# Expert gate and up projections turned over: weight blocks stationary, routed tokens streamed, in the mixture-of-experts stage of a two-layer decoder

## Chip, cores and metric

The kernel runs on one core of one Trainium2 chip. The metric is the device time of one execution in microseconds (us); lower is better. Before the change the median of three runs is 1061.97 us (1061.96 to 1063.9).

## What is computed

256 tokens of width 1024 pass through two layers, all in float32. Each layer has a token mixer (three attention branches and an output projection) and a feed-forward part. In layer 0 that is a dense SwiGLU of width 2816, in layer 1 a choice of two out of eight SwiGLU experts of width 1408. Only the expert stage is touched by the change:

```python
h = rms_norm(x, norm2_g[1])
logits = h @ w_router                       # 256 x 8
top_v, top_i = lax.top_k(logits, 2)
top_p = softmax(top_v)
combine = sum(one_hot(top_i, 8) * top_p[..., None], axis=1)
for e in range(8):
    out += combine[:, e:e+1] * ((silu(h @ w_gate[e]) * (h @ w_up[e])) @ w_down[e])
```

`w_gate` and `w_up` are 1024 x 1408 for each expert, `w_down` is 1408 x 1024. The eight experts hold 138.4 MB of weights.

## The kernel before

The mixer and the dense stage split each operand into a high and a low part of type float32r (three products instead of one) and take two thirds of the time. They are not changed. Then the router's logits are computed (two products per 128-row block, the token block stationary and 8 columns streamed), DVE turns them into slot numbers, and the expert stage begins.

**Passes.** The expert stage does two experts at a time, a heavy one with up to `HEAVY` = 96 token slots and a light one with up to `LIGHT` = 64. A loop with a count computed on the chip takes further passes if an expert has more tokens than slots; the kernel runs `STATIC` = 2 passes unrolled, then a loop, then the last pass written out by itself. With these inputs there are four passes.

**Gather.** `gather` (PE, line 1958) multiplies the 0/1 matrix `sel` (token to slot) with the token rows, kept as float32r high and low parts: 32 matmuls, each with a 128x128 block of the rows stationary and 160 slots streamed. ACT (`gathered`, line 918) copies the result to `xe`, feature-major, with the norm's gain.

**Gate and up.** `hidden(half, q, i)` (PE, line 1989) runs over two halves of the expert width (704 columns) and four pairs of 128-row blocks of the model width. The tokens are stationary and the weights are streamed. `quads` (line 1983) gives each of four 32-column strips of the array a group of 32 slots, so that four matmuls run side by side, each streaming 352 weight columns:

```python
for g in range(4):
    ins = plain(ps[g * OV:(g + 1) * OV, bank, 0:w], lhsT[:, g * OV:(g + 1) * OV], rhs[g // 2], first, last)
```

That covers 128 of the 160 slots. The last 32 slots of the heavy expert (the overflow) are four more strips, over 384 and 320 weight columns. ACT applies the SiLU with the norm factor of each slot as its scale (`gated`), DVE multiplies with the up product and again the factor. The products lie slot-major in `ehid` and `ehid2`.

**Turns.** The down projection needs them feature-major. `turn0` (line 2030) does 12 transposes on PE (8 of products, 4 of `sel`), `turn1` (line 2049) nine more; DVE copies them to `ehT`, `ehT2`, `selT`.

**Down and scatter.** `down` (line 2087) has 32 slots stationary and 512 weight columns streamed, again as quads. The result is scaled by the combine weight, split in high and low, and `scatter` (line 1972) adds it to the tokens by matmuls with `selT`; it runs in the first steps of the next pass (in pass 0 it runs on zeros). In the last pass all of the left output half (`h` = 0) is computed ahead of most of the right half, so that its scaling and scatter lie beside matmuls.

**Weights.** SP issues every weight load into one ring, `e_ring`, of three chunks (half a pass). A load waits for `e_used`, which PE raises after each step of `hidden` and `down`. A gate or up unit is 704 KB, a down unit 512 KB. The first 24 units are loaded during the mixer.

A matmul on plain float32 appears in the trace as two records, each with its own weight load (LDWEIGHTS, "PEld") and matmul; one on float32r appears as one.

Of the kernel before, what the change touches and what calls it, by code (L numbers as in the profile page):

```python
# [27 lines left out]
P = 128  # L28
# [173 lines left out]
HEAVY, LIGHT = 96, 64  # L202
OV = HEAVY - LIGHT
SLOTS = HEAVY + LIGHT
LISTED = 8
POSITIONS = NE + LISTED
WANT = (0, 5, 1, 4, 2, 3)
HALF_E = FE // 2
SLAB = HALF_E // 2
OV_SLAB = 384  # L210
OV_CUTS = (((0, 384, 0), (384, 320, 0)), ((0, 320, 64), (320, 384, 0)))
TURNED = 5
# [11 lines left out]
CHUNK = 8 * 2 * HALF_E  # L224
# [4 lines left out]
def e_place(u):  # L229

    turn, at = (0, u) if u < 24 else (1, u - 24)
    if turn == 0 or at < 8:
        chunk, j, size = at // 8, at % 8, 2 * HALF_E
    else:
        chunk, j, size = 1 + (at - 8) // FET, (at - 8) % FET, D
    if chunk == 2:
        return CHUNK_AT[2] + CHUNK - size * (j + 1), size
    return CHUNK_AT[chunk] + size * j, size


def e_before(u):

    a, n = e_place(u)
    here = [v for v in range(len(E_UNITS)) if (v < 24) != (u < 24) and e_place(v)[0] < a + n and a < sum(e_place(v))]
    return max(here)


E_FREE_LATER = (((0, 1, 2, 3, 4, 5, 16, 17), "v"), ((6, 7, 8, 9, 10, 11, 12, 13, 14, 15), "y"), ((18, 19), "wo"),
                ((20, 21), "router"), ((22, 23), "counts"))


E_GROUP = [u // 4 for u in range(len(E_UNITS))]
# [45 lines left out]
def build(nc, t):  # L298
    with ExitStack() as ctx:
# [28 lines left out]
        def expert_buffers():  # L328
# [5 lines left out]
                "ehid": sb("ehid", [FE]), "ehid2": sb("ehid2", [OV_SLAB]),  # L334
                "ehT": sb("ehT", [FET, P]), "ehT2": sb("ehT2", [FET, OV]),
                "y_hi": sb("y_hi", [D], F32R), "y_lo": sb("y_lo", [D], F32R),
                "y2": sb("y2", [2, HALF], F32R),
                "sg": sb("sg_e", [2, SLAB]), "sg2": sb("sg2_e", [OV_SLAB]),
# [21 lines left out]
        pslots, pscale = sb("pslots", [TT, POSITIONS + 2]), sb("pscale", [TT, POSITIONS + 2, 4], F32R)  # L360
# [63 lines left out]
        ehid, ehid2, ehT, ehT2 = eb["ehid"], eb["ehid2"], eb["ehT"], eb["ehT2"]  # L424
        y_hi, y_lo, y2 = eb["y_hi"], eb["y_lo"], eb["y2"]
        sg_e, sg2_e = eb["sg"], eb["sg2"]
# [3 lines left out]
        spare_sg = sg_e[:, :, :].rearrange("p a b -> p (a b)")  # L430
# [26 lines left out]
        loaded_e = [sem(f"loaded_e{i}") for i in range(len(E_UNITS) // 2)]  # L457
# [22 lines left out]
        turn0_filled, turn0_read = sem("turn0_filled"), sem("turn0_read")  # L480
        turn1_filled, turn1_read = sem("turn1_filled"), sem("turn1_read")
# [19 lines left out]
        def e_unit(u):  # L501

            _, _, _, k, _, c = E_UNITS[u]
            at, size = e_place(u)
            return e_ring[:, at:at + size].rearrange("p (k c) -> p k c", k=k)

# [50 lines left out]
        def _(sp):  # L557
# [10 lines left out]
            def expert_load(u, experts):  # L568
                which, e, k0, k, c0, c = E_UNITS[u]
                src = block_of(t["experts"][experts[e]], expert_at[which, k0, k, c0, c], k, c)  # L570
                sp.dma_start(e_unit(u), src).then_inc(loaded_e[u // 2], 16)
# [3 lines left out]
            for n, (src, k, w) in enumerate(static_units):  # L575
                if n == early_at:
                    sp.wait_ge(aux_done, FIRST[1, ("V3", 0)][2] + 2)
                if early_at <= n < early_at + len(free_later["v"]):
                    expert_load(free_later["v"][n - early_at], (0, 1))
# [25 lines left out]
            for u in range(24, len(E_UNITS)):  # L605
                sp.wait_ge(e_used, E_GROUP[e_before(u)] + 1)
                expert_load(u, (0, 1))
            sp.wait_ge(route_ready, 1)
            iters = sp.value_load(ids[0:1, POSITIONS:POSITIONS + 1], min_val=NE // 2, max_val=POSITIONS // 2)
            with sp.Fori(1, iters) as i:  # L610
                experts = [sp.value_load(ids[0:1, bass.ds(i * 2 + e, 1)], min_val=0, max_val=NE - 1) for e in range(2)]
                for u in range(len(E_UNITS)):
                    at = E_GROUP[e_before(u)] + 1 - (E_GROUPS if u < 24 else 0)
# [10 lines left out]
        def _(pool):  # L624
# [54 lines left out]
            pool.wait_ge(w_used, UNITS0)  # L679
            pool.memset(one[:, :, :], 0.0)  # L680
            for at, r in enumerate(WANT):
                pool.memset(want[:, at:at + 1], float(r))
            pool.memset(selT[:, :, :].bitcast(F32), 0.0)
            pool.memset(y_hi[:, :].bitcast(F32), 0.0)
            pool.memset(y_lo[:, :].bitcast(F32), 0.0)
            pool.memset(y2[:, :, :].bitcast(F32), 0.0).then_inc(moe_zero, 1)
# [9 lines left out]
        def _(act):  # L696
# [221 lines left out]
            def gathered(i):  # L918

                for g in range(3):  # L920
                    act.wait_ge(xe_filled, i * 3 + g + 1)
                    for k in range(3 * g, min(3 * g + 3, KD)):
                        at = (k - 3 * g) * SLOTS
                        ins = act.activation(xe[:, k, :], ps[:, 2 + g, at:at + SLOTS], ACT.Copy,
                                             scale=gain[:, 3 * KD + k:3 * KD + k + 1])
                    ins.then_inc(xe_ready, 1)

            gathered(0)
            act.wait_ge(diff_ready, 1)
            act.activation(ti[:, 5, :], ti[:, 4, :], ACT.Exp).then_inc(e_ready, 1)  # L930
            act.wait_ge(iters_ready, 1)
            last = act.value_load(ids[0:1, POSITIONS + 1:POSITIONS + 2], min_val=NE // 2 - 1, max_val=POSITIONS // 2 - 1)

            def gated(i):

                act.wait_ge(scale_ready, i + 1)
                for half in range(2):
                    for s in range(2):
                        act.wait_ge(hid_filled, i * 4 + 2 * half + s + 1)
                        act.activation(sg_e[:, s, :], ps[:, 2 * s, 0:SLAB], ACT.Silu, scale=slot_scale[:, 1:2]).then_inc(sg_ready, 1)  # L940
                    act.wait_ge(e_used, i * E_GROUPS + KQ * (half + 1))
                    act.activation(sg2_e[2 * OV:4 * OV, :], ps[0:2 * OV, 4, 0:OV_SLAB], ACT.Silu,
                                   scale=slot_scale[0:2 * OV, 3:4]).then_inc(sg_ready, 1)

# [11 lines left out]
            def full_pass(i):  # L956

                gated(i)
                gathered(i + 1)
# [6 lines left out]
            for i in range(STATIC):  # L966
                full_pass(i)
            with act.Fori(STATIC, last) as i:
# [3 lines left out]
            sqrt_table()  # L972
            act.wait_ge(y_filled, last * 2 + 1)
# [7 lines left out]
            act.activation(ehid[:, 0:HALF], ps[:, 6, :], ACT.Copy, scale=slot_scale[:, 0:1]).then_inc(y_hi_ready, 1)  # L981
# [14 lines left out]
        def _(dve):  # L996
# [328 lines left out]
            for n in range(3):  # L1325
                dve.memset(spare[:, n:n + 1], 0.0).then_inc(y_split, 1)
            for n in range(2):
                dve.memset(spare[:, 3 + n:4 + n], 0.0).then_inc(turn1_read, 1)
# [15 lines left out]

            def select(slot):

                dve.tensor_tensor(sel[:, :, 0:P].rearrange("p t (e c) -> p t e c", e=2),
                                  iota[:, 1:LIGHT + 1].unsqueeze(1).unsqueeze(1).broadcast_to([P, TT, 2, LIGHT]),
                                  slot(0, 2).unsqueeze(3).broadcast_to([P, TT, 2, LIGHT]), ALU.is_equal)
                dve.tensor_tensor(sel[:, :, P:2 * P].rearrange("p t (g c) -> p t g c", g=4),  # L1350
                                  iota[:, LIGHT + 1:HEAVY + 1].unsqueeze(1).unsqueeze(1).broadcast_to([P, TT, 4, OV]),
                                  slot(0, 1).unsqueeze(3).broadcast_to([P, TT, 4, OV]), ALU.is_equal).then_inc(sel_ready, 1)

# [4 lines left out]
            select(lambda n, w: eslot[:, :, n:n + w])  # L1358
# [4 lines left out]
            mean_square(3)  # L1363

# [10 lines left out]
            link(dve.tensor_scalar(heavy, rank, 2.5, float(OV), ALU.is_lt, ALU.mult))  # L1375
# [34 lines left out]


            dve.wait_ge(mean_sq, 4)
            rsqrt(nrm[:, 4, :], nrm[:, 3, :], nrm[:, 5, :], root, 4)
            scale18 = nrm[:, 4, :].unsqueeze(2).broadcast_to([P, TT, POSITIONS + 2])
            link(dve.tensor_copy(pscale[:, :, :, 2], scale18))
            link(dve.tensor_tensor(pscale[:, :, :, 3], scale18, pscale[:, :, :, 2].bitcast(F32), ALU.subtract))
# [42 lines left out]
            dve.wait_ge(iters_ready, 1)  # L1459
            last = dve.value_load(ids[0:1, POSITIONS + 1:POSITIONS + 2], min_val=NE // 2 - 1, max_val=POSITIONS // 2 - 1)  # L1460

# [9 lines left out]
            def scales(i):  # L1471

                dve.wait_ge(scale_filled, i + 1)
                for rows, dst, at in ((slice(0, LIGHT), 0, 0), (slice(LIGHT, P), 0, 4), (slice(0, P), 2, 8)):
                    ins = dve.tensor_reduce(slot_scale[rows, dst:dst + 2].unsqueeze(2),
                                            ps[rows, 6, at:at + 4].rearrange("p (v s) -> p v s", s=2), AX.X, ALU.add)
# [3 lines left out]
            def hidden(i, half):  # L1480

                c0 = half * HALF_E
                for s in range(2):
                    dve.wait_ge(sg_ready, i * 6 + 3 * half + s + 1)
                    dve.scalar_tensor_tensor(out=ehid[:, c0 + s * SLAB:c0 + (s + 1) * SLAB], in0=ps[:, 2 * s + 1, 0:SLAB],
                                             scalar=slot_scale[:, 1:2], in1=sg_e[:, s, :],
# [714 lines left out]
```

## Time and profile before

| | before |
|---|---|
| median of 3 runs | 1061.97 us |
| the profiled execution, its own time | 1068.14 us |
| its span | 1066.4 us |
| PE busy / PE weight loads busy | 1050.6 us (99%) / 867.3 us (81%) |
| DVE busy / ACT busy | 518.9 us (49%) / 402.5 us (38%) |
| mean granted TensorE clock | 0.983 of full |
| read from memory | 252.93 MB |

The span runs from the first to the last instruction. PE's busy time is a union of overlapping matmuls whose ends are modelled, so 99% says that PE always had something in flight, not that it ran at its peak. The weight loads are listed as an engine of their own since they overlap the matmuls. A granted clock of 1.00 is 2.4 GHz, one of 0.50 is 1.2 GHz.

### The profile page before, as it was taken

The page shows a single profiled execution, that of the slowest core. Times are in us where ns is not written, and L with a number is a line of the kernel's source. Part 1 is how long each engine was busy: PE and PEld are TensorE (multiplying, and loading weights), DVE is VectorE, ACT ScalarE, POOL GpSimd, SP SyncE. Part 2 cuts the span into 40 slices and gives each one's busy share as a digit, 9 for nine tenths or more (in the row PEclk, how much of TensorE's full clock was granted, in tenths as well). Part 3 has the DMA queues.
Part 4 walks back from the last instruction along what each step waited for, and adds up shares of the span by engine and source line. Part 5 has one row for each costly group of instructions (what it writes and reads, how often), then busy time and mean ns, then how long its engine had stood idle before and what let it go on. Part 6 is the DMA issues. An engine that isn't in the chain of part 4 may idle for free.

```text
span 1066.4 us, 21967 instructions
## 1 busy us (share of the span) xinstructions
PE 1050.6 (99%) x9653; PEld 867.3 (81%) x9653; DVE 518.9 (49%) x751; ACT 402.5 (38%) x619; POOL 16.2 (2%) x61
## 2 busy tenths in 40 slices
PE   7999999999999999999999999999999999999996
PEld 7998999999999999999899999995654554563552
DVE  4566676577467565465577755954112111111112
ACT  5553655636354353447356564431111011011012
POOL 3000000000000000000000000010000000000000
PEclk8999999999999999999999999988999999999998
DMA  6543543556455465454435348895999999999961
GB/s 213 173 154 93 177 157 137 171 188 204 152 179 184 153 221 189 167 172 155 138 106 191 131 130 308 311 386 212 406 414 414 409 413 414 411 411 415 411 271 40
DMA packets 56910, 255.38 MB, mean 239 GB/s; under 512 B 7505, under 2 KB 7537, under 8 KB 56818
## 3 DMA queue, kind: packets, MB, share of 16 engines
q1 hardware_dynamic: 55954, 252.41, 64.5%
q8 instruction: 76, 1.25, 0.5%
q10 hardware_dynamic: 864, 1.59, 0.4%
q14 instruction: 16, 0.13, 0.0%
HBM read 252.93 MB, written 1.05 MB: 238 GB/s over the span
## 4 chain that ended last, share of the span: by engine, by line
PE 95%; DMA 2%; DVE 1%; ACT 1%; issue 0%; ACTq 0%; DVEq 0%
PE ps L1603 37%; PE ps L1598 16%; PE ps L1600 16%; PE ps L1599 16%; PE ps L1592 3%; PE ps L1594 3%; PE ps L1593 3%; DMA raw<-in_dense 1%; PE ps L1811 1%; DMA x<-in_x 1%; ACT w_hi L708 0%; DVE w_lo L1008 0%; PE ps L2036 0%; PE ps L2045 0%; PE ps L2053 0%
## 5 line engine op out<-in xcount | busy, mean ns | idle before, releaser
L1008 DVE TENSOR_TENSOR w_lo<-raw,w_hi 128x1536 fp32r<-128x1536 f32 (+2 forms) x157 | 248.1, 1604 | 128.6 <-ACT w_hi L708 128.4
L708 ACT ACTIVATE w_hi<-raw 128x1536 fp32r<-128x1536 f32 (+2 forms) x157 | 210.4, 1361 | 155.4 <-DMA raw<-in_dense 153.5
L1598 PE MATMUL ps<-hT_hi,w_hi 128*128 128x256 f32 (+1 forms) x752 | 216.3, 288 | 4.2 <-DVE hT_lo L1057 4.2
L1600 PE MATMUL ps<-hT_hi,w_lo 128*128 128x256 f32 (+1 forms) x752 | 213.0, 283 | 0.0
L1599 PE MATMUL ps<-hT_lo,w_hi 128*128 128x256 f32 (+1 forms) x752 | 212.9, 283 | 0.0
L1603 PE MATMUL ps<-e_ring,xe 128*32 128x352 f32 (+2 forms) x2560 | 199.9, 463 | 0.0
L1603 PEld LDWEIGHTS ps<-e_ring,xe 128*32 128x32 f32 x2560 | 106.1, 110 | 83.5 <-issue 56.2
L1598 PEld LDWEIGHTS ps<-hT_hi,w_hi 128*128 128x128 f32 (+1 forms) x752 | 142.4, 189 | 8.5 <-issue 7.6
L1600 PEld LDWEIGHTS ps<-hT_hi,w_lo 128*128 128x128 f32 (+1 forms) x752 | 142.4, 189 | 0.4
L1599 PEld LDWEIGHTS ps<-hT_lo,w_hi 128*128 128x128 f32 (+1 forms) x752 | 142.2, 189 | 0.4
L1603 PE MATMUL ps<-e_ring,ehT 128*32 128x512 f32 x880 | 101.1, 593 | 0.0
L1598 PE MATMUL ps<-h_hi,w_hi 128*128 128x256 f32 x352 | 100.1, 284 | 0.6 <-DVE w_lo L1008 0.6
L1600 PE MATMUL ps<-h_hi,w_lo 128*128 128x256 f32 x352 | 99.1, 282 | 0.0
L1599 PE MATMUL ps<-h_lo,w_hi 128*128 128x256 f32 x352 | 99.0, 281 | 0.0
L1603 PEld LDWEIGHTS ps<-e_ring,ehT 128*32 128x32 f32 x880 | 32.8, 110 | 59.3 <-issue 53.8
L940 ACT ACTIVATE sg_e<-ps,slot_scale 128x352 f32<-128x352 f32 x16 | 8.9, 553 | 168.5 <-PE ps L1603 168.5
L1598 PEld LDWEIGHTS ps<-h_hi,w_hi 128*128 128x128 f32 x352 | 67.0, 190 | 0.8 <-DVE w_lo L1008 0.8
L1599 PEld LDWEIGHTS ps<-h_lo,w_hi 128*128 128x128 f32 x352 | 66.9, 190 | 0.0
L1600 PEld LDWEIGHTS ps<-h_hi,w_lo 128*128 128x128 f32 x352 | 66.9, 190 | 0.0
L1592 PE MATMUL ps<-w_hi,hT_hi 128*128 128x256 f32 (+1 forms) x208 | 64.6, 311 | 0.1
L1594 PE MATMUL ps<-w_hi,hT_lo 128*128 128x256 f32 (+1 forms) x208 | 63.9, 307 | 0.0
L1593 PE MATMUL ps<-w_lo,hT_hi 128*128 128x256 f32 (+1 forms) x208 | 63.7, 306 | 0.0
(330 smaller groups left out, 1419.4 us busy)
## 6 DMA issues: line engine op xcount, KB each, us to landing
e_ring<-in_experts SPq DMA_DIRECT2D x128, 704.0 KB, 11.5
raw<-in_dense SPq DMA_DIRECT2D x112, 768.0 KB, 4.3
e_ring<-in_experts SPq DMA_DIRECT2D x88, 512.0 KB, 10.3
raw<-in_dense SPq DMA_DIRECT2D x42, 512.0 KB, 3.6
raw<-in_dense SPq DMA_DIRECT2D x3, 544.0 KB, 3.9
raw<-in_dense SPq DMA_DIRECT2D x2, 272.0 KB, 3.6
x<-in_x ACTq DMA_DIRECT2D x2, 256.0 KB, 6.6
x<-in_x SPq DMA_DIRECT2D x1, 512.0 KB, 8.6
```

The source lines that it names most:

```text
L708: act.activation(slot(n, "hi", k), slot(n, "raw", k), ACT.Copy).then_inc(hi_done, 1)
L940: act.activation(sg_e[:, s, :], ps[:, 2 * s, 0:SLAB], ACT.Silu, scale=slot_scale[:, 1:2]).then_inc(sg_ready, 1)
L1008: dve.tensor_tensor(slot(n, "lo", k), slot(n, "raw", k), slot(n, "hi", k).bitcast(F32), ALU.subtract).then_inc(lo_done, 1)
L1592: pe.matmul(out, hi, wh, start=first, stop=False, skip_group_check=True)
L1593: pe.matmul(out, hi, wl, start=False, stop=False, skip_group_check=True)
L1594: return pe.matmul(out, lo, wh, start=False, stop=last, skip_group_check=True)
L1598: pe.matmul(out, wh, hi, start=first, stop=False, skip_group_check=True)
L1599: pe.matmul(out, wh, lo, start=False, stop=False, skip_group_check=True)
L1600: return pe.matmul(out, wl, hi, start=False, stop=last, skip_group_check=True)
L1603: return pe.matmul(out, lhsT, rhs, start=start, stop=stop, skip_group_check=True)
L1811: ins = pe.transpose(aux_bank(a + hh)[:, blk * P:(blk + 1) * P], sm[:, at:at + P], ident[:, :])
```

## The change

Gate and up are turned over. A unit of weights now holds, for one expert and one half, 2 row blocks of 11 column blocks of 128: five gate blocks, five up blocks, and one block that is half gate and half up (64 columns each). Each block is the stationary operand, and the slots of that expert are streamed: 84 for the heavy one, 64 for the light one. The products come out feature-major, so they need no turn. `HEAVY` falls from 96 to 84 and the slots from 160 to 148.

```diff
-HEAVY, LIGHT = 96, 64
-OV = HEAVY - LIGHT
+HEAVY, LIGHT = 84, 64
+OV = 32
+GATED = FE // P // 2
+GU = (2 * GATED + 1) * P
...
-        E_UNITS += [(which, e, 2 * _q, 2, HALF_E * _h, HALF_E) for which in ("gate", "up") for e in range(2)]
+        E_UNITS += [("hidden", e, 2 * _q, 2, _h, GU) for e in range(2)]
...
             def hidden(half, q, i):
-                for s in range(2):
...
-                        for kk, k in enumerate(ks):
-                            ins = quads(2 * s + kind, SLAB, xe[:, k, 0:P], [units[2 * kind + e][:, kk, cols] for e in range(2)],
-                                        k == 0, k == KD - 1)
...
+                for e in range(2):
+                    n, at = WIDTH[e], AT[e]
+                    u = (half * KQ + q) * 2 + e
+                    weights = e_unit(u)
+                    if half == 1 and q == 0:
+                        pe.wait_ge(hid_ready, i * 4 + e + 1)
+                    expert_ready(u, i)
+                    for kk in range(2):
...
+                        for b in range(2 * GATED + 1):
+                            bank, j = (2 * e + 1, b - GATED) if GATED <= b < 2 * GATED else (2 * e, min(b, GATED))
+                            ins = plain(ps[:, bank, j * n:(j + 1) * n], weights[:, kk, b * P:(b + 1) * P], xe[:, k, at:at + n],
+                                        k == 0 and j == 0, k == KD - 1)
```

The norm factor of a token no longer enters at the SiLU. After the first of its three groups, `gather` does two more float32 matmuls that put the factor of each slot on all partitions (`r_rows` times `sel`), and the copy to `xe`, now on DVE, multiplies by it:

```diff
+                    if g == 0:
+                        if first:
+                            pe.wait_ge(r_ready, 1)
+                        for tt in range(TT):
+                            ins = plain(ps[:, 1, 0:SLOTS], r_rows[:, tt, :], sel[:, tt, 0:SLOTS].bitcast(F32), start=tt == 0, stop=tt == TT - 1)
+                        ins.then_inc(r_filled, 1)
```

Of the turns only the four transposes of `sel` stay (`turn`, before step (1, 1)); `turn0` and `turn1` go. ACT applies the SiLU to five blocks at once and to the half block, DVE multiplies straight into `ehT`:

```diff
-                ins.then_inc(turn1_filled, 1)
...
+            def turn(i, first):
+
+                if not first:
+                    pe.wait_ge(added, i * 4 + 4)
+                pe.wait_ge(sel_all, i + 1)
+                for part in range(2):
+                    for tt in range(TT):
+                        ins = pe.transpose(ps[:, 7, (2 * part + tt) * P:(2 * part + tt + 1) * P],
+                                           sel[:, tt, part * P:(part + 1) * P].bitcast(F32), ident[:, :])
+                ins.then_inc(turn_filled, 1)
```

Three smaller edits go with it. Pass 0 has no scatter and no add of rows any more. In the last pass the two output halves are computed side by side, and the last block decides both:

```diff
-            for k in range(4):
+            for k in range(FET):
                 down_ready(k, last)
                 down_main(k, 0)
-            turn1(last)
-            for k in range(4):
+                if k == FET - 1:
+                    down_over((k,)).then_inc(y_filled, 1)
                 down_main(k, 1)
...
+                if k < FET - 1:
+                    down_over((k,))
+            pe.wait_ge(y_split, last * 3 + 2)
```

And SP issues a pass's gate and up weights as 16 loads of 1408 KB instead of 32 of 704 KB; the bytes are the same. In the mixer these early loads stand at every second dense load.

## Rows read from the trace of the kernel before

**Rows 1.** The page: span, busy time by engine, GB/s in 40 slices.

```profile
span 1066.4 us, 21967 instructions
...
PE 1050.6 (99%) x9653; PEld 867.3 (81%) x9653; DVE 518.9 (49%) x751; ACT 402.5 (38%) x619; POOL 16.2 (2%) x61
...
GB/s 213 173 154 93 177 157 137 171 188 204 152 179 184 153 221 189 167 172 155 138 106 191 131 130 308 311 386 212 406 414 414 409 413 414 411 411 415 411 271 40
```

**Rows 2.** The page's DMA issues: count, KB each, us to landing.

```profile
e_ring<-in_experts SPq DMA_DIRECT2D x128, 704.0 KB, 11.5
...
e_ring<-in_experts SPq DMA_DIRECT2D x88, 512.0 KB, 10.3
```

**Rows 3.** Chain that ended last, in order: start us, us, engine, line.

```profile
867.17 57.77 PE ps L1603 x614
...
950.19 57.77 PE ps L1603 x614
```

**Rows 4.** Timeline of PE in pass 0: start us, us, line, operands, records.

```profile
723.03 7.85 PE L1603 MATMUL ps<-e_ring,xe 128*32 128x352 f32 x80
...
730.81 0.51 PE L1603 MATMUL ps<-y_hi,selT 128*128 128x512 f32 x1
...
733.11 6.22 PE L1603 MATMUL ps<-e_ring,xe 128*32 128x352 f32 x80
```

**Rows 5.** The same view, later in pass 0.

```profile
739.26 0.50 PE L1603 MATMUL ps<-y_hi,selT 128*128 128x512 f32 x1
...
740.16 6.22 PE L1603 MATMUL ps<-e_ring,xe 128*32 128x352 f32 x80
746.31 0.61 PE L1603 MATMUL ps<-pscale,sel 128*128 128x8 f32 x4
746.85 12.04 PE L1603 MATMUL ps<-e_ring,xe 128*32 128x352 f32 x160
758.82 0.66 PE L2036 MATMUL ps<-ident,ehid 128*128 128x128 f32 x4
...
760.43 17.63 PE L1603 MATMUL ps<-e_ring,xe 128*32 128x352 f32 x236
...
782.93 0.66 PE L2053 MATMUL ps<-ident,ehid 128*128 128x128 f32 x4
...
784.07 4.50 PE L1603 MATMUL ps<-e_ring,ehT 128*32 128x512 f32 x40
788.50 3.80 PE L1603 MATMUL ps<-sel,rows 128*128 128x160 f32 x32
792.23 15.21 PE L1603 MATMUL ps<-e_ring,ehT 128*32 128x512 f32 x137
```

**Rows 6.** Timeline: runs of matmuls with 128 stationary columns.

```profile
709.36 2.31 PEld L1603 LDWEIGHTS ps<-r_gain,xhat 128*128 128x128 f32 x20
709.46 2.30 PE L1603 MATMUL ps<-r_gain,xhat 128*128 128x8 f32 x20
...
716.01 7.09 PE L1603 MATMUL ps<-sel,rows 128*128 128x160 f32 x32
```

**Rows 7.** Sums by stretch; PEclk is the first number after the engines.

```profile
700.00:712.00 12.00, 12.00 (x102) 12.00 (x102) 4.29 (x15) 5.01 (x15) 3.48 (x11) 1.00 0.98 381
712.80:722.80 10.00, 10.00 (x49) 10.00 (x48) 8.14 (x47) 2.13 (x7) 0.00 (x0) 0.50 0.91 347
722.80:726.40 3.60, 3.60 (x26) 1.28 (x29) 1.96 (x13) 2.16 (x4) 0.00 (x0) 0.51 0.03 13
726.40:740.00 13.60, 13.60 (x152) 6.44 (x144) 5.63 (x20) 0.00 (x0) 0.00 (x0) 1.00 0.55 214
...
790.00:792.00 2.00, 2.00 (x20) 2.00 (x20) 0.00 (x0) 1.52 (x5) 0.00 (x0) 1.00 1.02 417
```

**Rows 8.** Timeline of ACT in the tail of the last pass.

```profile
1054.88 0.69 ACT L981 ACTIVATE ehid<-ps,slot_scale 128x512 f32<-128x512 f32 x1 [1.30 <-PE ps L1603]
```

More of the change, by code:

```diff
@@ L199 @@
 BANKS = 4
-HEAVY, LIGHT = 96, 64
-OV = HEAVY - LIGHT
+HEAVY, LIGHT = 84, 64
+OV = 32
 SLOTS = HEAVY + LIGHT
+WIDTH = (HEAVY, LIGHT)
+AT = (LIGHT, 0)
 LISTED = 8
@@ L243, in e_before @@
     a, n = e_place(u)
-    here = [v for v in range(len(E_UNITS)) if (v < 24) != (u < 24) and e_place(v)[0] < a + n and a < sum(e_place(v))]
+    here = [v for v in range(len(E_UNITS)) if (v < TURN) != (u < TURN) and e_place(v)[0] < a + n and a < sum(e_place(v))]
     return max(here)
-E_FREE_LATER = (((0, 1, 2, 3, 4, 5, 16, 17), "v"), ((6, 7, 8, 9, 10, 11, 12, 13, 14, 15), "y"), ((18, 19), "wo"),
-                ((20, 21), "router"), ((22, 23), "counts"))
-E_GROUP = [u // 4 for u in range(len(E_UNITS))]
+E_FREE_LATER = (((0, 1, 2, 8), "v"), ((3, 4, 5, 6, 7), "y"), ((9,), "wo"), ((10,), "router"), ((11,), "counts"))
+E_GROUP = [u // 2 if u < DOWN_AT else (u - DOWN_AT) // 4 + DOWN_AT // 2 for u in range(len(E_UNITS))]
 E_GROUPS = E_GROUP[-1] + 1
@@ L456, in build @@
         loaded = [sem(f"loaded{i}") for i in range(RING)]
-        loaded_e = [sem(f"loaded_e{i}") for i in range(len(E_UNITS) // 2)]
+        loaded_e = [sem(f"loaded_e{i}") for i in range(DOWN_AT + FET)]
         hi_done, lo_done, w_used = sem("hi_done"), sem("lo_done"), sem("w_used")
@@ L604, in _ @@
                 expert_load(u, (0, 1))
-            for u in range(24, len(E_UNITS)):
+            for u in range(TURN, len(E_UNITS)):
                 sp.wait_ge(e_used, E_GROUP[e_before(u)] + 1)
@@ L972, in _ @@
             sqrt_table()
+            act.wait_ge(scale_ready, last + 1)
             act.wait_ge(y_filled, last * 2 + 1)
@@ L1322, in _ @@
                         split_lo(u)
[L1325 to L1328, printed above, removed]
+            for n in range(4):
+                dve.memset(spare[:, n:n + 1], 0.0).then_inc(added_filled, 1)
+                dve.memset(spare[:, n + 4:n + 5], 0.0).then_inc(added, 1)
             a = ROUTER_AUX
@@ L1342, in _, with matches @@
             rows_lo(2)
-            def select(slot):
[L1347 to L1352, printed above, removed]
+            def matches(first, n, out, slots):
+                shape = list(out.shape)
+                numbers = iota[:, first:first + n].unsqueeze(1)
+                if len(shape) == 4:
+                    numbers, slots = numbers.unsqueeze(1), slots.unsqueeze(3)
+                return dve.tensor_tensor(out, numbers.broadcast_to(shape), slots.broadcast_to(shape), ALU.is_equal)
+            def select(slot):
+                matches(1, HEAVY, sel[:, :, LIGHT:SLOTS], slot(0))
+                matches(1, LIGHT, sel[:, :, 0:LIGHT], slot(1)).then_inc(sel_ready, 1)
+                matches(LIGHT + 1, HEAVY - LIGHT, sel[:, :, P + OV:2 * P].rearrange("p t (g c) -> p t g c", g=3)[:, :, :, 0:HEAVY - LIGHT],
+                        slot(0)).then_inc(sel_all, 1)
             a += 1
@@ L1480, in hidden @@
             def hidden(i, half):
[L1482 to L1486, printed above, removed]
-                                             op0=ALU.mult, op1=ALU.mult).then_inc(hid_ready, 1)
-                dve.wait_ge(sg_ready, i * 6 + 3 * half + 3)
@@ L1549, in _ @@
             add_rows(last)
+            hidden(last, 0)
+            turned(last)
             scales(last)
-            hidden(last, 0)
-            turned0(last)
             hidden(last, 1)
-            turned1(last)
             dve.wait_ge(y_hi_ready, last * 4 + 1)
@@ L1980, in expert_ready @@
             def expert_ready(u, i):
-                pe.wait_ge(loaded_e[u // 2], i * 32 + 32)
+                per_pass = 16 if u < DOWN_AT else 32
+                pe.wait_ge(e_loaded(u), i * per_pass + per_pass)
             def quads(bank, w, lhsT, rhs, first, last):
                 for g in range(4):
-                    ins = plain(ps[g * OV:(g + 1) * OV, bank, 0:w], lhsT[:, g * OV:(g + 1) * OV], rhs[g // 2], first, last)
+                    ins = plain(ps[g * OV:(g + 1) * OV, bank, 0:w], lhsT[:, g * OV:(g + 1) * OV], rhs[1 - g // 2], first, last)
@@ L2093, in down, with first_half, second_half @@
                 down_over(k_pair(q)).then_inc(e_used, 1)
-            def first_half(i):
-                pe.wait_ge(turn1_read, i * 2 + 2)
+            def first_half(i, first=False):
                 hidden(0, 0, i)
-                pe.wait_ge(y_split, i * 3 + 3)
-                for g in range(3):
-                    scatter(g)
+                if not first:
+                    pe.wait_ge(y_split, i * 3)
+                    for g in range(3):
+                        scatter(g)
                 hidden(0, 1, i)
-                pe.wait_ge(added, i * 4 + 1)
-                scatter(3)
+                if not first:
+                    pe.wait_ge(added, i * 4 + 1)
+                    scatter(3)
                 hidden(0, 2, i)
+                hidden(0, 3, i)
+            def second_half(i, first=False):
+                hidden(1, 0, i)
+                turn(i, first)
                 pe.wait_ge(scale_known, 1)
                 slot_scales(i)
-                hidden(0, 3, i)
-            def second_half(i):
-                hidden(1, 0, i)
-                turn0(i)
                 hidden(1, 1, i)
@@ L2166, in _ @@
                 out, tokens = ps[:, LAST_BANKS[1][tt], :], slice(tt * P, (tt + 1) * P)
-                plain(out, selT[:, 0, tokens].bitcast(F32), ehid[:, 0:HALF], stop=False)
+                plain(out, selT[:, 0, tokens].bitcast(F32), y_last[:, :], stop=False)
                 plain(out, selT[:, 1, tokens], y2[:, 1, :], start=False).then_inc(added_filled, 1)
@@ L2188, with gate_up @@
     laid["dense"] = np.concatenate([cut(given[w][l], *block) for w, l, *block in dense_blocks()])
-    laid["experts"] = np.stack([np.concatenate([cut(given["moe_w_" + w][0, e], *block) for w, *block in expert_blocks()]) for e in range(NE)])
+    def gate_up(e, h):
+        gate, up = given["moe_w_gate"][0, e], given["moe_w_up"][0, e]
+        wide, narrow = slice(GATED * P * h, GATED * P * (h + 1)), slice(2 * GATED * P + 64 * h, 2 * GATED * P + 64 * (h + 1))
+        return np.concatenate([gate[:, wide], up[:, wide], gate[:, narrow], up[:, narrow]], axis=1)
+    laid["experts"] = np.stack([np.concatenate([cut(gate_up(e, h), k0, k, 0, c) if w == "hidden" else cut(given["moe_w_down"][0, e], k0, k, h, c)
+                                                for w, k0, k, h, c in expert_blocks()]) for e in range(NE)])
     laid["x"] = np.asarray(inputs["x"])[0].T.reshape(KD, P, T).transpose(1, 0, 2)
```

266 lines of the change are left out of this document (105 added, 161 removed).

## The prediction

> **What bounds the kernel now.** I read the page first. PE has work in flight for 1050.6 of 1066.4 us, DVE and ACT for half or less [rows 1]; so only PE's own time counts, unless memory does. In the last third of the span the memory moves 406 to 415 GB/s without a dip [rows 1], which asks whether the expert stage is bound by its loads. The chain that ended last answers: one down stage begins at 867.17 and the next at 950.19, so a pass takes 83.0 us, and the chain runs through PE alone [rows 3]. The loads of a pass are 32 of 704 KB and 22 of 512 KB [rows 2], 34.6 MB, and 34.6 MB in 83.0 us are 417 GB/s. PE and memory are in balance: a faster PE would soon run into its loads, a slower one just stretches the pass.
>
> I then add up PE's pass from the timeline, to see that no wait hides in it. A step of `hidden` (80 records) takes 6.15 us, from 733.11 to 739.26 [rows 4, 5] and again from 740.16 to 746.31; two take 11.97 us, three 17.46 us (760.43 to about 777.9) [rows 5]. Three single steps, the two and the three make 8 steps and 47.9 us. The turns take 1.61 us (758.82 to 760.43) and 1.14 us (782.93 to 784.07), the slot scales 0.54 us, the gather 3.73 us (788.50 to 792.23) [rows 5]. The scatters take 2.30 us (730.81 to 733.11) and 0.90 us (739.26 to 740.16) [rows 4, 5]. The down projection has 220 records, 40 of them take 4.43 us (784.07 to 788.50) [rows 5], so 24.4 us. The sum is 82.5 us of 83.0: PE waits for nothing.
>
> **The step that decides: what one record of the new gate and up costs.** The new `hidden` has per pass 2 halves x 8 row blocks x 11 column blocks x 2 experts = 352 matmuls in float32, which are 704 records, each with a load of 128 stationary columns of its own. The old one has 640 records with 32 stationary columns, four side by side. So I look for runs of records with 128 stationary columns at full clock. With 8 columns streamed, 20 records start over 2.30 less one record's length of about 0.25 us: 19 steps, 0.108 us each, at a clock of 1.00 [rows 6, 7]. With 160 streamed, 32 records take 3.73 us, 0.117 us each to the next instruction or 0.113 us between their own starts (3.80 less about 0.3, over 31) [rows 5], also at 1.00 [rows 7]. Twenty times as many streamed columns cost 5 to 9 ns: the load of 128 stationary columns sets the pace, not the stream. The new records stream 84 or 64 float32 columns. An old step has 20 groups of four records, with 7168 columns one behind the other (16 x 352 and 4 x 384) in 6.15 us, so at most 0.86 ns a column; 84 columns are then 0.072 us and 64 are 0.055 us, both below 0.108. So a new record takes between 0.108 us (8 columns) and 0.117 us (160 columns); I take 0.111. A pass has 704 x 0.111 = 78.1 us in place of 47.9.
>
> The Trainium skill (TensorE: Matmul & The Clock Gate, section Back-to-back issue gap) gives about 81 ns per matmul for a sustained stream of load and matmul pairs with 128 streamed columns. By that a pass would have 704 x 0.081 = 57.0 us and the change would cost far less. The rows disagree, 0.108 us even with 8 columns, and the same page (section Weight-path perf modes) says that the fast weight load is not used for FP32. It stands below as a rival.
>
> **The clock.** At half clock the same load takes twice as long: the first gather's 32 records take 7.09 us, 0.215 us from start to start (7.09 less about 0.43, over 31) [rows 6], at 0.50 [rows 7]. It fell at 712.8, behind the logits with their 8 columns and the short waits around them [rows 6, 7]. From there the gather runs without a break to 722.8 and the clock stays at 0.50; with 3.6 us of quads it is back at 1.00 [rows 7]. The new `hidden` starts right behind this gather, and its records are of the gather's kind: a load of 128 columns each, and a stream that is shorter than the load. So I take it that in pass 0 it stays at half clock to its end, and that the down quads bring the clock back. In pass 0's second gather the same kind of records ran for 3.7 us from full clock, and it stayed at 1.00 [rows 5, 7]. So I take the later passes at full clock, with less certainty: their `hidden` lasts 78 us, not 3.7.
>
> **The sum.** Against the profiled span of 1066.4 us (own time 1068.14), which the median of the runs shown, 1061.97, undercuts by 6.2 us; I add the difference to the median.
>
> Pass 0. Removed: `hidden`, whose first step took 7.78 us (723.03 to 730.81) since part of it ran at half clock [rows 4], so 49.5; the scatters on zeros, 3.2; of the turns 8 of 12 transposes and all of the second, 1.07 + 1.14 = 2.2. Together 54.9. Added: 704 x 0.215 = 151.4; the factor's 4 records, 1.0 at half clock; the four transposes and slot scales at half clock, 1.1 more; the first part of the down projection at half clock, 2.5 (bounds 1.7 to 3.6, from the 3.6 us that quads needed [rows 7]). Net +101.1. Before it, the factor's records stand in the gather: +1.1; the copies to `xe` are now DVE's, about 0.3 us each behind the last group, and only the first group is waited for at once.
> Passes 1 and 2, each: 78.1 + 0.5 (factor) - 47.9 - 2.2 = +28.5, together +57.0.
> Last pass: 78.1 - 47.9 - 2.2 = +28.0.
> Tail. Before, scaling, split and scatter of the left half lay beside the right half's matmuls; the last scaling on ACT (0.69 us) began at 1054.88 and 11.5 us led from it to the end [rows 8]. Now some seven such operations stand between the last down block and that point, with 1 us of matmuls left beside them: +4 (2 to 6).
> Sum: 101.1 + 1.1 + 57.0 + 28.0 + 4.0 = +191 us, so 1253 us.
>
> At no cost: SiLU and products, since each of them has the other expert's records of a step (44 x 0.111 = 4.9 us) beside it before PE needs the bank or `ehT`; without that cover about 1.5 us for each of four per pass. The next pass's `select` and the copies to `xe` lie beside the down projection, with some 15 us to spare. The loads: 34.6 MB in 111 us are 312 GB/s, so PE no longer meets them; loads twice as large in the mixer could hold a dense load up once or twice (0 to 2 us). More passes would come if an expert had more tokens than slots, but the reference's router gives 71, 53, 72, 58, 59, 66, 59 and 74 tokens, with 84 slots for each of four and 64 for the others: four passes as before.
>
> **Rivals.**
> (a) The clock returns soon in pass 0. For it: PE has no pause in `hidden`. Against: nor has the gather. Pass 0 then has 78.1 + 0.5 + 3.5 (its first 7 us at half clock) - 54.9 = +27.2; total 27.2 + 1.1 + 57.0 + 28.0 + 4.0 = +117, 1179 us. Chance 0.14.
> (b) The clock falls in passes 1 to 3 too, where 64 columns are streamed, and stays down to the end of `hidden`. For it: the fall at 712.8 followed records with few columns. Against: the warm gather. Each of three passes has 73.3 + about 6 (scatters, turn, first quads) more than above: +429, 1491 us. Chance 0.10; a fall in some passes only, 1290 to 1450, another 0.05.
> (c) The loads hide behind the stream, and a record takes its stream: 352 x 0.072 + 352 x 0.055 = 44.7 us a pass, -4.9 us with the turns and the factor. This ends on the other side. The place is every `hidden` step, and it decides below (47.9 + 2.2 - 0.5) / 704 = 0.070 us a record. PE alone would give about 1042 us (-9.7 + 1.1 - 2 x 4.9 - 5.4 + 4.0); as memory already moves what 83 us need, more likely 1050 to 1062. Against: the rows with 128 stationary columns are all at 0.108 us or more. Chance 0.02.
> (d) A record takes 0.081 us, by the page named above: 57.0 + 0.5 - 50.1 = +7.4 a pass. With pass 0 at twice that (0.162) the total is about +91, 1153 us; all at full clock, about 1095. Chance 0.02.
> The forecast has 0.67, its own range 1235 to 1275: +-5 ns on the 2112 records at full clock is 10 us, the rest waits and tail.
>
> **How the numbers follow.** The likeliest case gives 1253. To hold the time 8 times in 10 the range takes in (a): low 1170, high 1285. That leaves out (b), (c) and (d) and the partial falls, 0.19. This measurement can tell about 0.2%, 2 us. Only (c) is near or under the old time: faster 0.01, same 0.01, slower 0.98.
>
> **What the profile of the changed kernel would show.** The record spacing: groups of 44 records of `ps<-xe,e_ring` with 128 stationary columns, 4.9 us each, PE's weight loads busy throughout. The clock: 0.50 from about 713 to 876, then 1.00; a pass distance of about 111 us; memory near 312 GB/s in passes 1 to 3. Wrong would be a spacing under 0.105, a clock of 1.00 within pass 0's `hidden`, or 0.50 in later ones.

## The result, and the profile after

The changed kernel is slower: 1174.06 us in the median of five runs against 1062.46 us, a ratio of 1.103 with a 95% interval of 1.100 to 1.106. The forecast was 1253 us with a range of 1170 to 1285. Its runs lie on two levels: two of the five took 1251.34 and 1253.14 us, three took 1173.15 to 1174.06, and the ratio is made from the latter. The profiled execution is one of the former, 1253.14 us with a span of 1251.4. What separates the levels is the subject of most of the experiments.

The page of the changed kernel: span, busy time, the granted clock in tenths and the memory rate in 40 slices.

```profile
span 1251.4 us, 22172 instructions
...
PE 1232.5 (98%) x9845; PEld 1139.5 (91%) x9845; DVE 514.2 (41%) x765; ACT 389.9 (31%) x595; POOL 13.3 (1%) x59
...
PEclk8999999999999999999999855555999999999998
...
GB/s 207 177 119 160 147 133 180 177 198 178 178 152 219 178 165 165 144 133 144 146 220 319 370 125 102 177 137 140 331 317 270 345 356 257 296 344 345 277 102 34
```

Against [rows 1], the weight loads on PE rise from 867 to 1140 us, and memory no longer stands at 406 to 415 GB/s in the expert stage: it moves 102 to 177 GB/s in pass 0 and swings between 257 and 356 in the passes behind it. Five slices at half clock, which the kernel before did not have, follow the router.

The timeline of PE in the changed kernel (start us, us, line, operands, records), pass by pass:

```profile
723.56 94.06 PE L1594 MATMUL ps<-xe,e_ring 128*128 128x84 f32 x440
817.41 1.06 PE L2026 MATMUL ps<-ident,sel 128*128 128x128 f32 x4
...
818.98 56.56 PE L1594 MATMUL ps<-xe,e_ring 128*128 128x84 f32 x264
875.47 10.59 PE L1594 MATMUL ps<-e_ring,ehT 128*32 128x512 f32 x80
...
905.79 10.04 PE L1594 MATMUL ps<-xe,e_ring 128*128 128x84 f32 x88
...
928.33 29.59 PE L1594 MATMUL ps<-xe,e_ring 128*128 128x84 f32 x264
957.76 0.60 PE L2026 MATMUL ps<-ident,sel 128*128 128x128 f32 x4
...
1016.70 10.04 PE L1594 MATMUL ps<-xe,e_ring 128*128 128x84 f32 x88
...
1127.62 10.04 PE L1594 MATMUL ps<-xe,e_ring 128*128 128x84 f32 x88
```

The line of records says 84 columns for both experts, since rows are merged by operands. In pass 0 the 704 records of gate and up run from 723.56 to 817.41 and from 818.98 to 875.47, 150.3 us, 0.2135 us each. In a later pass 264 records take 29.43 us (928.33 to 957.76), 0.1115 us each. The passes begin at 905.79, 1016.70 and 1127.62: 110.9 us apart, against 83.0 in [rows 3].

The sums by stretch of the same kernel (engines' busy time, then granted clock, DMA share, GB/s):

```profile
700.00:712.00 12.00, 12.00 (x104) 12.00 (x104) 4.86 (x20) 5.02 (x15) 0.97 (x9) 1.00 0.97 390
712.00:724.00 12.00, 12.00 (x57) 12.00 (x57) 5.83 (x25) 1.49 (x2) 0.00 (x0) 0.50 0.78 297
...
840.00:860.00 20.00, 20.00 (x95) 20.00 (x95) 0.00 (x0) 0.00 (x0) 0.00 (x0) 0.50 0.50 180
860.00:880.00 20.00, 20.00 (x101) 16.58 (x104) 2.29 (x7) 1.40 (x4) 0.00 (x0) 0.52 0.44 171
880.00:900.00 20.00, 20.00 (x188) 8.61 (x180) 2.79 (x9) 0.00 (x0) 0.00 (x0) 1.00 0.78 306
...
940.00:960.00 20.00, 20.00 (x182) 20.00 (x182) 2.63 (x8) 1.40 (x4) 0.00 (x0) 1.00 0.81 296
```

The clock stands at half from 712 to the end of pass 0's gate and up, and is back a few us into the down quads (which start at 875.47). In the later passes it stays at full.

### The profile page after: what moved, and what is told of

The parts are those of the page before. It is cut to its first block, busy times and chain, and to the rows that moved or that the text cites. A ratio compares the mean times of both kernels' runs of the same rounds, so it can differ in the third digit from the quotient of the medians.

```text
span 1251.4 us, 22172 instructions
## 1 busy us (share of the span) xinstructions
PE 1232.5 (98%) x9845; PEld 1139.5 (91%) x9845; DVE 514.2 (41%) x765; ACT 389.9 (31%) x595; POOL 13.3 (1%) x59
## 4 chain that ended last, share of the span: by engine, by line
PE 94%; DVE 2%; DMA 2%; ACT 1%; issue 0%; ACTq 0%; DVEq 0%
PE ps L1594 47%; PE ps L1589 14%; PE ps L1591 13%; PE ps L1590 13%; PE ps L1583 2%; PE ps L1585 2%; PE ps L1584 2%; DMA raw<-in_dense 1%; DVE w_lo L999 1%; PE ps L1802 1%; DMA x<-in_x 1%; ACT w_hi L709 0%; DVE xhat L1256 0%; DVE pT L1253 0%; PE ps L2026 0%
## 5 line engine op out<-in xcount | busy, mean ns | idle before, releaser
L1594 PEld LDWEIGHTS ps<-xe,e_ring 128*128 128x128 f32 x2816 | 387.7, 227 | 3.0 <-issue 2.5
L1594 PE MATMUL ps<-xe,e_ring 128*128 128x64 f32 (+1 forms) x2816 | 388.3, 312 | 0.0
L930 ACT ACTIVATE sg_e<-ps 128x420 f32<-128x420 f32 (+1 forms) x16 | 7.7, 479 | 376.8 <-PE ps L1594 376.8
L1492 DVE TENSOR_TENSOR ehT<-ps,sg_e 128x420 f32<-128x420 f32 (+1 forms) x16 | 8.7, 544 | 258.2 <-ACT sg_e L930 258.2
L1594 PEld LDWEIGHTS ps<-e_ring,ehT 128*32 128x32 f32 x880 | 29.4, 111 | 64.2 <-issue 63.6
```

The lines of the kernel that those rows point to most:

```text
L930: act.activation(sg_e[:, e, 0:w], ps[:, 2 * e, 0:w], ACT.Silu).then_inc(sg_ready, 1)
L1492: dve.tensor_tensor(ehT[:, GATED * half:GATED * (half + 1), at:at + n], ps[:, 2 * e + 1, 0:w].rearrange("p (b c) -> p b c", b=GATED), sg_e ...
L1594: return pe.matmul(out, lhsT, rhs, start=start, stop=stop, skip_group_check=True)
```

## The experiments

**The two levels.** The changed kernel ran again, unchanged.

> The changed kernel once more. In the five runs so far it took 1251 to 1253 us twice and 1173 to 1174 us three times. Theory (clock): the two levels are one kernel with the first pass's gate and up stage at half or at full clock; if its profile is of a run near 1174, the records of all four passes are 0.112 us apart and the granted clock is 1.00 from about 700 us to the tail; if near 1252, it is 0.50 from about 712 to 879. Rival: the short runs save the 78 us in many places (waits, transfers), and then the record spacing in the first pass is 0.21 us in both.

Eight runs, each with its time and its mean granted clock over the span:

```
1252.48 0.927   1252.02 0.925   1251.66 0.926
1174.70 0.992   1173.33 0.992   1173.97 0.995   1173.02 0.992   1175.18 0.992
```

Ratio of the short ones to the kernel before 1.104 (1.101 to 1.107). In all thirteen runs, these and the first five, a long run has a mean clock of 0.924 to 0.927 and a short one of 0.992 to 0.995, so the level goes with the clock. A mean clock c over a span S leaves 2 x (1 - c) x S at half clock: 2 x 0.074 x 1250 = 185 us in a long run, 2 x 0.008 x 1172 = 19 us in a short one. The difference, 166 us, is the stretch from 712 to 879 in the windows above; a short run has no room for more than a few us of it. The profiled execution fell on the long level again, so the trace of a short one as such was not seen; the trace of the third experiment shows pass 0 at full clock. The 704 records of pass 0 alone account for 704 x (0.2135 - 0.1115) = 71.8 of the 78 us between the levels; the rest lies in the gather ahead of them and in the first down quads.

**Make the clock fall.** The changed kernel without the idle matmuls that fill PE's waits around the choice of experts:

```diff
-            keep_busy(proj_bank(FIRST[1, ("wo", 0)][1]), 6)
...
-            keep_busy(proj_bank(FIRST[1, ("wo", 0)][1]), 4)
```

> The changed kernel without the ten idle matmuls on ident that fill PE's waits between the logits and the gather; nothing computed is left out. Theory: the clock then always falls ahead of the gather, and since the records of gate and up are load-bound it does not return before the down stage: every run at 1250 to 1255 us, no run near 1174. Rival: the clock returns by itself within some us of the gate and up stage, and the long runs had another cause: most runs near 1174 to 1185.

Measured: 1251.41 us in the median, all four runs between 1250.80 and 1252.73, mean clock 0.925 to 0.928: four runs of four on the long level, where the kernel with these matmuls had five of thirteen. Its windows show where:

```profile
708.00:710.00 2.00, 2.00 (x21) 2.00 (x20) 1.47 (x11) 1.18 (x5) 0.00 (x0) 1.00 0.84 315
710.00:712.00 2.00, 0.51 (x6) 0.44 (x5) 1.34 (x6) 0.00 (x0) 0.00 (x0) 0.70 0.96 366
...
726.00:740.00 14.00, 14.00 (x67) 14.00 (x67) 7.53 (x41) 1.49 (x2) 0.00 (x0) 0.50 0.01 2
```

PE idles from 710.5 on, the clock falls, and the 67 records of gate and up in the last stretch have no pause and do not bring it back. That the idle time itself is the trigger is not shown by this: in the changed kernel's own trace PE was in flight for all of 700 to 712, and the clock fell at about 711.9 all the same, behind the logits' records with 8 streamed columns.

**Bring the clock back.** Four dense matmuls, eight records, between the first gather and the first step; their result is not used:

```diff
             gather(first=True)
+            for _ in range(4):
+                plain(ps[:, 5, :], ident[:, :], x[:, 0, 0:HALF])
```

> The changed kernel with four float32 matmuls of 512 streamed columns (8 records, results unused) between the first gather and the first gate and up step. Theory: a dense stretch brings the clock back as the quads did before, so every run is short: 1176 to 1182 us (1174 plus 3.4 us of records at full clock, up to 6.8 at half clock and the half-clock gather), and none near 1252. Rival: the clock's fall is not undone by so short a stretch: some or all runs at 1255 to 1260.

Measured: 1182.04 us in the median, six runs of 1178.46 to 1185.18 (three above the 1182 expected), none on the long level. The clock fell here before the gather in the profiled run, and then:

```profile
712.00:722.00 10.00, 10.00 (x48) 10.00 (x48) 4.55 (x20) 1.49 (x2) 0.00 (x0) 0.50 0.85 331
722.00:727.00 5.00, 5.00 (x14) 2.57 (x14) 3.62 (x23) 0.00 (x0) 0.00 (x0) 0.76 0.00 0
727.00:740.00 13.00, 13.00 (x118) 13.00 (x117) 7.35 (x39) 1.49 (x2) 0.00 (x0) 1.00 0.17 52
```

The timeline of PE in this kernel has pass 0 at full clock:

```profile
722.66 4.49 PE L1594 MATMUL ps<-x,ident 128*128 128x512 f32 x8
726.99 49.24 PE L1594 MATMUL ps<-xe,e_ring 128*128 128x84 f32 x440
776.07 0.61 PE L2026 MATMUL ps<-ident,sel 128*128 128x128 f32 x4
```

The 440 records that took 93.85 us take 49.08 here (726.99 to 776.07), 0.1115 us each, as in the later passes. Eight dense records of 4.3 us are worth 70 us to a run on the long level. Five of the six runs took 1181.39 us or more at a mean clock of 0.984 to 0.989, so the clock had fallen ahead of the burst there, as in the trace; the sixth took 1178.46 at 0.992, 4.4 us more than a short run of the changed kernel, which is the burst itself.

**The price of a record.** The same kernel as the changed one, but each record of gate and up streams 32 slots instead of 84 or 64 (the other slots are not computed):

```diff
-                            ins = plain(ps[:, bank, j * n:(j + 1) * n], weights[:, kk, b * P:(b + 1) * P], xe[:, k, at:at + n],
+                            ins = plain(ps[:, bank, j * n:j * n + 32], weights[:, kk, b * P:(b + 1) * P], xe[:, k, at:at + 32],
```

> The changed kernel with 32 slots streamed per record in gate and up in place of 84 and 64, the other slots not computed. Theory (the load of 128 stationary columns sets the pace): records 0.108 to 0.110 us apart at full clock, so 0 to 3 us less per pass, a run 0 to 12 us under the changed kernel at the same clock (1162 to 1174, or 1240 to 1253 with the clock down in the first pass; with fewer columns it may fall more often or in more passes). Rival (stream plus load, or stream alone): 42 columns less on average, 84 cycles of 0.42 ns, 0.035 us per record, 25 us per pass, 99 us in all: about 1075.

Measured: 1455.28 us, 281 us more than the changed kernel's median, for less work. The time missed all the numbers expected, since the clock did what the expectation had only named as possible: it fell in every pass. The page shows it in 40 slices, with full clock only around the down stages:

```profile
PEclk9999999999999999999955558555595555855558
```

The 2816 records of gate and up, nearly all of them at half clock, cost 0.102 us more each; that is 287 us if it were all of them, so the clock accounts for the 281. The windows show pass 0 start at full clock this time and fall within the first records:

```profile
718.00:720.00 2.00, 2.00 (x21) 2.00 (x19) 1.91 (x9) 0.00 (x0) 0.00 (x0) 1.00 0.99 389
...
722.00:726.00 4.00, 4.00 (x26) 4.00 (x25) 3.41 (x22) 0.00 (x0) 0.00 (x0) 0.62 0.03 7
726.00:740.00 14.00, 14.00 (x67) 14.00 (x67) 4.78 (x25) 1.49 (x2) 0.00 (x0) 0.50 0.37 137
```

The price of a record can still be read, at the same clock on both sides. The timeline, here in pass 1 at half clock:

```profile
994.00 56.51 PE L1594 MATMUL ps<-xe,e_ring 128*128 128x32 f32 x264
1050.44 10.57 PE L1594 MATMUL ps<-e_ring,ehT 128*32 128x512 f32 x80
```

264 records with 32 columns take 56.44 us; 264 records with 84 and 64 take 56.49 us in pass 0 of the changed kernel (818.98 to 875.47). The streamed columns cost nothing, 0.214 us a record at half clock with either number. Nor is it a fixed price of any record: the old ones, with 32 stationary columns and 352 streamed, start 0.077 us apart (80 in 6.15 us, [rows 4, 5]). That leaves the load of 128 stationary columns, as the theory has it; the rival (99 us less through fewer columns) is out. The comparison is at half clock; at full clock the evidence is the rows with 8, 84 or 64, and 160 columns.

**The same fall in the kernel before.** Its ten idle matmuls left out in the same way:

> The kernel before without the ten idle matmuls on ident between the logits and the gather; nothing computed is left out. Theory: the clock falls ahead of the gather in every run, here too, but the quads bring it back within some us, so it costs little: 1064 to 1070 us against 1059 to 1067. Rival: the fall is as dear here as in the changed kernel (78 us), about 1140.

Measured: 1065.59 us in the median of ten runs (1063.71 to 1068.46) beside 1063.85 (1060.82 to 1067.62) for the kernel before; ratio 1.0016 (1.0001 to 1.0032). The windows of this kernel:

```profile
716.00:722.00 6.00, 6.00 (x34) 4.89 (x37) 5.05 (x31) 3.36 (x9) 0.00 (x0) 0.50 0.68 277
722.00:726.00 4.00, 4.00 (x52) 1.59 (x48) 2.81 (x16) 0.73 (x2) 0.00 (x0) 0.87 0.02 4
726.00:740.00 14.00, 14.00 (x160) 6.69 (x152) 4.39 (x11) 0.00 (x0) 0.00 (x0) 1.00 0.71 264
```

The clock falls and the quads bring it back. The 19 runs of the kernel before in that comparison show the same two cases: seven at a mean clock of 0.992 or more with a median of 1062.2 us, twelve at 0.989 or less with 1065.6, which is also what the kernel without idle matmuls takes. So the fall costs the kernel before 3.4 us, and with the new gate and up it costs 78. In this trace the clock was already down before PE had its first pause at 709.64:

```profile
709.40:709.60 0.20, 0.20 (x2) 0.14 (x1) 0.00 (x0) 0.00 (x0) 0.00 (x0) 0.50 1.05 422
```

**The tail.** The third experiment's kernel, with the last pass in the order of the kernel before:

```diff
             for k in range(FET):
                 down_ready(k, last)
                 down_main(k, 0)
-                if k == FET - 1:
-                    down_over((k,)).then_inc(y_filled, 1)
+            for q in range(DQ):
+                ins = down_over(k_pair(q))
+            ins.then_inc(y_filled, 1)
+            for k in range(8):
                 down_main(k, 1)
-                if k < FET - 1:
-                    down_over((k,))
             pe.wait_ge(y_split, last * 3 + 2)
             for tt in range(TT):
                 scatter(2 * tt, LAST_BANKS[0][tt])
+            for k in range(8, FET):
+                down_main(k, 1)
```

> The changed kernel with the four dense matmuls of the run before and, in the last pass, the order of the kernel before: the left output half of all eleven down blocks, the overflow, eight blocks of the right half, the scatter of the left half, three more blocks. Theory: the tail was the 4 us of the forecast (2 to 6), so 1176 to 1180 against 1178 to 1185 for the same kernel without this. Rival: the wait at the end lies beside nothing and the order costs the same either way: no difference.

Measured: 1179.59 us (1178.58 to 1180.10), 2.5 us less. The medians alone do not settle it, since the intervals of the two ratios to the kernel before overlap (1.109 to 1.115 and 1.106 to 1.111); the traces do. The timelines, first of the kernel with the tail of the change, then with the old order (in brackets: idle time before, and what ended it):

```profile
1139.22 24.23 PE L1594 MATMUL ps<-e_ring,ehT 128*32 128x512 f32 x220
1164.95 0.50 PE L1594 MATMUL ps<-y_hi,selT 128*128 128x512 f32 x1 [1.50 <-DVE y L1513]
...
1168.88 1.13 PE L1594 MATMUL ps<-y_last,selT 128*128 128x512 f32 x2 [2.25 <-ACT y_last L972]
```

```profile
1140.28 21.66 PE L1594 MATMUL ps<-e_ring,ehT 128*32 128x512 f32 x196
1161.87 0.50 PE L1594 MATMUL ps<-y_hi,selT 128*128 128x512 f32 x1
...
1163.47 2.78 PE L1594 MATMUL ps<-e_ring,ehT 128*32 128x512 f32 x24
1167.06 1.13 PE L1594 MATMUL ps<-y_last,selT 128*128 128x512 f32 x2 [0.81 <-ACT y_last L972]
```

Two waits, 1.50 and 2.25 us, become one of 0.81: 2.9 us in the traces, from the start of the down stage to the end (40.4 against 37.5 us). The forecast's term was 4.

**One part of the change alone, in the kernel before.** Pass 0 without its scatters and without the adds that belong to them:

```diff
-                pe.wait_ge(y_split, i * 3 + 3)
-                for g in range(3):
-                    scatter(g)
+                if not first:
+                    pe.wait_ge(y_split, i * 3 + 3)
+                    for g in range(3):
+                        scatter(g)
```

> The kernel before with one part of the change alone: no scatter on zeros and no add of rows in the first pass. Theory: PE is the bound there, so the 3.2 us of the scatters go: 1056 to 1060 on runs in which the clock did not fall. Rival: the loads of the expert stage are the bound, and the time stays within 1 us.

Measured: 1059.48 us in the median of eight runs, against 1063.85; ratio 0.9950 (0.9930 to 0.9969). Its runs lie between 1055.78 us at a mean clock of 0.993 and 1063.49 at 0.983. This small edit is faster than the kernel before, by 4.4 us in the medians where the scatters on zeros took 3.2, so the rival is out. At like clocks the gain is 3.4 us (0.983) to 6.3 (0.993, two runs); what gives more than the 3.2 was not looked into.

**Is memory the next bound of the kernel before?** Its overflow matmuls of gate and up, cut to 64 columns each (the heavy expert's last 32 slots are then not computed); the loads stay as they are:

```diff
-                    for w, s in sorted((OV_CUTS[half][s][1], s) for s in range(2)):
-                        c0, _, at = OV_CUTS[half][s]
-                        for kind in range(2):
-                            g = 2 * kind + s
-                            ins = plain(ps[g * OV:(g + 1) * OV, 4, at:at + w], xe[:, k, P:SLOTS],
-                                        units[2 * kind][:, kk, c0:c0 + w], k == 0, k == KD - 1)
+                    for g in range(4):
+                        ins = plain(ps[g * OV:(g + 1) * OV, 4, 0:64], xe[:, k, P:SLOTS], units[0][:, kk, 0:64], k == 0, k == KD - 1)
```

> The kernel before with the overflow matmuls of gate and up cut from 8 of 384 or 320 columns per row block pair to 8 of 64, so that the heavy expert's last 32 slots are not computed. PE has about 1.2 us less per step, 9 us less per pass (74 us); the loads are the same 34.6 MB. Theory (memory and PE in balance): the loads now set the pass at 82 to 84 us (415 GB/s), PE waits for them, and the kernel gains under 10 us: 1050 to 1060. Rival (memory follows PE and has room): 74 us a pass at 465 GB/s, 36 us less, about 1026.

Measured: 1056.14 us (1055.63 to 1059.13), ratio 0.9925 (0.9899 to 0.9950). Four transposes of `sel` mark the passes in its timeline:

```profile
755.21 0.66 PE L2041 MATMUL ps<-ident,sel 128*128 128x128 f32 x4
...
829.93 0.66 PE L2041 MATMUL ps<-ident,sel 128*128 128x128 f32 x4
...
904.65 0.66 PE L2041 MATMUL ps<-ident,sel 128*128 128x128 f32 x4
...
987.59 0.66 PE L2041 MATMUL ps<-ident,sel 128*128 128x128 f32 x4
```

Twice a pass takes 74.7 us, PE's own time. Then one takes 82.9 us. The windows over the three passes say why (the second number from the end is the DMA share, the last GB/s):

```profile
755.00:830.00 75.00, 75.00 (x933) 34.42 (x934) 14.24 (x29) 8.64 (x18) 0.00 (x0) 1.00 1.02 413
830.00:905.00 75.00, 75.00 (x932) 34.49 (x933) 14.23 (x30) 8.64 (x18) 0.00 (x0) 1.00 1.02 412
905.00:988.00 83.00, 75.80 (x932) 33.60 (x930) 14.01 (x30) 8.64 (x18) 0.00 (x0) 1.00 1.02 412
```

Memory moves 412 or 413 GB/s in all three. In 74.7 us that is 30.8 MB of the 34.6 that a pass uses, and the difference comes out of the lead that the ring had from the loads made during the mixer, until it is spent. PE's weight loads wait for memory there, and the chain that ended last shows it too:

```profile
982.65 0.16 PEld L1603 LDWEIGHTS ps<-e_ring,xe 128*32 128x32 f32 x8 [3.02 <-DMA e_ring<-in_experts]
```

```profile
1016.14 15.70 DMA e_ring<-in_experts
1031.88 13.99 PE ps L1603 x113
```

8.3 us less per pass on PE, 33 us in four passes, gave 7.7 us in the whole kernel. So even if the forecast's rival (c) had held, with PE 4.9 us faster per pass than before, it would have brought little.

## Why the prediction was right, and where not

**The price of a record** was the step that decides, and it held. Forecast 0.111 us at full clock and 0.215 at half; measured 0.1115 and 0.2135, and at half clock the same with 32 columns as with 84 and 64. The two rivals with a cheaper record are out: (c), the stream alone (0.072 and 0.055 us), and (d), the 81 ns that the Trainium skill (TensorE: Matmul & The Clock Gate, section Back-to-back issue gap) gives for pairs with 128 streamed columns. The measured 111.5 ns has 84 or 64 float32 columns. One sum of rival (d) is off: by its own terms the case with all at full clock comes to 1091 us, not 1095.

**Passes at full clock.** Forecast +28.5 us each; the distance grew from 83.0 to 110.9, +27.9. The later passes stay at full clock, as forecast, and rival (b) is out for 84 and 64 columns. With 32 columns it came true.

**Pass 0 at half clock.** Forecast +101.1 and +1.1 ahead of it. In the profiled execution it runs from 723.56 to 905.79, 182.2 us. Of the kernel before, the first record of pass 1 is this row of the timeline of PE:

```profile
806.85 0.48 PE L1603 MATMUL ps<-e_ring,xe 128*32 128x352 f32 x1
```

From 723.03 [rows 4] that is 83.8 us, so +98.4, and +0.5 at the start. The last pass with the tail took 1251.4 - 1127.62 = 123.8 us against 93.5 (1066.4 less 806.85 and two passes of 83.0), +30.3 where 28 + 4 was forecast. The tail term was too large by 1.1 to 1.5 us, by the experiment on it. In all +185 on the span where +191 was forecast. For the execution that was profiled the working holds within 6 us. That 1253 meets the long level (1251 to 1253 us) to the microsecond is luck: the sum was 6 us too large, and it was added to a median 6 us below the execution that it was worked out from.

**The median is another case.** Here the step that failed is the one on the clock: "in pass 0 it stays at half clock to its end". Once the clock has fallen, that is so in all three traces of it: the two of the changed kernel and the one without idle matmuls, whose four runs are all long. But it rests on the fall at 712.8, which I read from one trace and took for certain, although the median of the runs was 6 us below that trace. In 8 of 13 runs the clock did not fall there, or only for a few us, by their mean clocks. Those took 1173 to 1175 us: 1179 was worked out for rival (a), which had 0.14. The number of (a) was nearly right, but not its reason. Under (a) the clock is down through the gather and 7 us more, some 19 us; in the trace with the burst it was down for 14 us around the gather (710.7 to 724.4), and that run has a mean clock of 0.989, so (a) would show about 0.987. The short runs have 0.992 to 0.995. So the forecast of 1253 was too high by 79 us for the median, one cause, and that the range held it is luck: it reached down to (a), a case that did not happen.

**At no cost.** SiLU, products, the second `select` and the copies to `xe` stayed hidden: the passes at full clock are 0.6 us shorter than forecast. Memory moved 314 and 313 GB/s in passes 1 and 2 (forecast 312), and PE never waited for it in passes 1 to 3. The balance of PE and memory in the kernel before is confirmed by the last experiment.

**What stays open.** What makes the clock hold or fall around the router was not found. Without the idle matmuls the changed kernel was on the long level in four runs of four, with them in five of thirteen; but the traces show the fall with PE in flight throughout, and once just ahead of the idle time, so the idle time is at most a part of the cause. No trace of a short run of the changed kernel was taken.

## What to carry to other kernels

Ask of each float32 matmul how long its stream is against its weight load: with 128 stationary columns a record costs 0.11 us here whether it streams 8 columns or 84 (or 160 in float32r), and four 32-column strips side by side with long streams beat it by far: 48 us a pass against 78. A stage made of such load-bound records kept the clock that it found with 84 and 64 columns, lost it with 32, and won it back with neither, so what a fall of the clock costs depends on the stage behind it: 3.4 us with quads, 78 with this. And if one trace shows a fall of the clock, look at the spread of the run times before taking it for certain.

## What the runs showed that was not expected

Less work made the kernel 281 us slower: with 32 streamed columns per record instead of 84 or 64 the records take the same time, but the granted clock, at 1.00 when the stage began, fell to 0.50 within 8 us (718 to 726), and the same came in each of the later passes. And a dense stretch of 4.3 us that computes nothing takes a run of the changed kernel from 1252 to 1182 us.
